# Placing a merge's output weights in a weight ring, splitting the first loads, and adding products of constants

## The chip, the cores and the metric

The kernel runs on one core of a Trainium2 chip. The metric is the device time of one execution in microseconds; before the change the median of three runs is 1440.2 us (1438.92 to 1441.64).

## The reference

One step of a decoder layer for 256 prompt tokens and 8 sample tokens (T = 264), width 1024, all in float32. What matters here are the end of the mixing part and the expert part:

```
h = rms_norm(x);  y_a = rwkv(h);  y_b = sparse_attention(h);  g_a, g_b = sigmoid gates of h
x = x + (g_a * (y_a @ w_br_a) + g_b * (y_b @ w_br_b)) @ w_out          # the merge
logits = rms_norm(x) @ w_router + b_router                             # 32 experts
top_val, top_e = top_k(logits, 4);  top_w = softmax(top_val)
for each expert e, over its tokens:
    u = h @ w_up[e] + b_up[e]                                          # 1024 x 2048
    y = clamped_swiglu(u) @ w_down[e] + b_down[e]                      # 1024 x 1024
    x += top_w * y
y = rms_norm(x)
```

The weights of an expert are 8 MiB (upper) and 4 MiB (lower); all 32 experts are always computed, on tiles of 64 token slots.

## The kernel before

The program is a row of blocks that end with a barrier of all engines: the input projection and the RWKV part, the attention (its setup, L928; the prompt, L1199; the samples, L1433), the merge (L1680) and the experts (L2099), with the routing at their head. Inside a block each engine has its own instruction stream, in program order, and waits on semaphores.

*The ring.* Expert weights go through eight buffers `pairs[0..7]` of 2 MiB (L175). Pairs 0 to 3 take the upper weights (two of the eight row tiles of 128 each), pairs 4 and 5 the lower weights of even experts, 6 and 7 those of odd experts. Pairs 4 to 7 lie in memory that is `sel` before: there the sample attention has its selected rows, and then the merge has the branch weights `w_br_a` and `w_br_b` in one half of the columns (0:128) and `w_out` in the other (128:256). All weight loads are issued by SP on one queue. `upper_weights(sp, 0)` (L183) issues the upper pairs of expert 0 in the merge; `down(0)` and `down(1)` (L1854) issue the lower pairs of experts 0 and 1 in the next block, behind the bias rows (L1858, L1859). From then on SP issues the upper pairs of expert e (L2110) as PE uses those of e-1, pair by pair (`up_used`, and `up_done` for the last), and the lower pairs (L2121) in the same way. The first issue of this kind, for expert 1, waits until PE has used pair 0 of expert 0.

*The merge.* SP issues eight loads of `w_out` (row c to `sel[:, c, ..., 128:256]`, in runs of 128 columns, 512 bytes), x again (L1702), seven constants (L1708) and the upper weights. POOL waits for all but the last of these and then issues the copy of the window cache, 4088 KB from HBM to HBM (L1718). PE computes the two branch products for eight column tiles (L1764, semaphore `ab`), then the output product (L1776, semaphore `od`) with x added through `twice` (L1778), then two sums for the router and the mean squares (L1784, L1789). DVE makes `mixed` (L1741 to L1743), the squares (L1749) and the last copy (L1751).

*The routing.* PE: two groups of products with `fold` (L2014), the transposes of all rows of x (L2022), the ranks (L2028, L2030), the first expert's rows picked by a product (L2036), the slot tables (L2043). DVE: logits, top 4, one-hot tables, `first_rows` (L1923), a wait for the bias rows and then the picked columns (L1931, L1932), and the gains of the first expert's rows (L1958). ACT writes the rows to a scratch tensor in HBM, 1.08 MB in all (L1879), from which POOL gathers each later expert's rows (L2161). Nothing of the first expert's upper product (L2417 bias, L2430 weights) waits for a gather.

*The experts.* PE does the upper product of e, the sums of e-1 or e-2 back onto the tokens (L2405), transposes of the next rows (L2387) and of h (L2393), the lower product (L2444 bias, L2451 weights). Up to expert 15 the lower product of e-1 stands behind the upper product of e, from 16 on that of e itself.

*Other places of the diff.* At the end of the RWKV part PE turns the last state (L896). In the attention's setup it transposes blocks of the cache (L1175), computes small setup products (L1146), the hidden layer of the compression (L1135), and after a wait for ACT's gelu the second layer (L1188, L1193). The attention of the prompt begins with 32 small products (L1347) and gate projections (L1356).

Of the kernel before, what the change touches and what calls it, by code (L numbers as in the profile page):

```python
# [29 lines left out]
P = 128  # L30
D = 1024
# [73 lines left out]
def build(nc, a, o, scratch):  # L105
    ctx = ExitStack()
    with ctx:
# [17 lines left out]
        def at(name, shape, place, dt=F32):  # L125
            return nc.alloc_sbuf_tensor_at(name, shape, dt, offset=place)
# [56 lines left out]
        def upper_weights(sp, e):  # L183
            for q in range(4):
                sp.dma_start(pairs[q][:], a["w_up"][0][e, 256 * q:256 * q + 256, :].rearrange("(p c) n -> p c n", c=2)).then_inc(ring_in[2 * q], 16)

# [31 lines left out]
        halves_of = (slice(0, HD), slice(HD, P))  # L218

# [403 lines left out]
        def rwkv_chunks(ar, q, bk, wc, av, br, vt, ktt, r, v):  # L623

            with nc.Block() as block, ExitStack() as st:
# [145 lines left out]
                def _(pe):  # L771
# [125 lines left out]
                    mm.then_inc(so, 1)  # L897

# [26 lines left out]
        def compress(sel, rows, qg, yb, B0, B1, gtok, bin_):  # L925

            with nc.Block() as block, ExitStack() as st:  # L928
# [196 lines left out]
                def _(pe):  # L1125
# [40 lines left out]
                    for b in range(NR // 2):  # L1166
                        if b % 2 == 0:
                            pe.wait_ge(C["raw_in"][b // 2], 32)
                        for r in (2 * b, 2 * b + 1):
                            if r >= 3:  # L1170
                                pe.wait_ge((fl_a, fl_d)[(r - 3) % 2], 2 * ((r - 3) // 2) + 1)
                            for kv in range(2):
                                for t in range(2):
                                    c0 = 256 * (r % 4) + P * kv
                                    mm = nc.tensor.transpose(banks[r % 3][:, TP * kv + P * t:TP * kv + P * t + P], raw[b // 2][:, t, c0:c0 + P], ident)  # L1175
                            mm.then_inc(turned, 1)
                        if 2 * b in at_half:
                            setup(at_half.index(2 * b))
                        if b:
                            layer1(2 * b - 2)  # L1180
                            layer1(2 * b - 1)
                        if 2 * b + 1 in at_half:
                            setup(at_half.index(2 * b + 1))
                    layer1(NR - 2)
                    layer1(NR - 1)
                    pe.wait_ge(gl_ok, 2)
# [7 lines left out]
                    mm.then_inc(vc, 1)  # L1194

# [482 lines left out]
        def merge(sel, br_in):  # L1678

            with nc.Block() as block, ExitStack() as st:  # L1680
# [11 lines left out]
                root_w = at("table_of_root", [P, 1], TEMPS)  # L1692
                wo_in, x_again = sem("mg_w_out_in"), sem("x_in_again")

                @block.sync
                def _(sp):
                    for c in range(KD):
                        sp.dma_start(sel[:, c, :, :, P:256], a["w_out"][0][P * c:P * c + P, :].rearrange("p (a b n) -> p a b n", a=2, b=4)).then_inc(wo_in, 16)
# [11 lines left out]
                    upper_weights(sp, 0)  # L1710
# [43 lines left out]
                def _(pe):  # L1754
# [15 lines left out]
                    for m in range(KD):  # L1770
                        if m >= 2:
                            pe.wait_ge(oe, m - 1)
                        for c in range(KD):
                            if m == 0 and c == KD - 1:
                                pe.wait_ge(mix_ok, KD)
                            mmul(banks[m % 2][:, 0:T], sel[:, c, m // 4, m % 4, P:256], mix[:, c, :], start=(c == 0), stop=False)  # L1776
# [13 lines left out]
                    mm.then_inc(partd, 1)  # L1790

# [24 lines left out]
        def route(st):  # L1816
# [33 lines left out]
            def sp_routes(sp):  # L1850
                def down(e):
                    for j in range(2):
                        slot = 8 + 4 * e + 2 * j
                        sp.dma_start(pairs[slot // 2][:], a["w_down"][0][e, 512 * j:512 * j + 512, :].rearrange("(p b c) n -> p b (c n)", b=2, c=2)).then_inc(ring_in[slot], 16)  # L1854

# [5 lines left out]
                down(0)  # L1861
                down(1)
# [147 lines left out]
            def pe_routes(pe):  # L2010
                mmul = nc.tensor.matmul
                for lo, signal in ((1, msd), (0, lgd)):
# [3 lines left out]
                    mm.then_inc(signal, 1)  # L2016
                for i in range(6):
# [13 lines left out]
                mm.then_inc(rkd, 1)  # L2031
                for t, (_, n) in enumerate(TILES):
# [543 lines left out]
```

## Time and profile before

| | |
|---|---|
| median of three runs | 1440.2 us |
| profiled execution, its own time | 1438.5 us |
| its span | 1436.6 us |
| PE busy | 1336.5 us, 93% of the span |
| DVE / ACT / POOL busy | 495.3 / 189.9 / 101.9 us |
| mean granted clock of TensorE | 0.974 |
| DMA | 479.94 MB, mean 334 GB/s |
| chain that ended last | DMA 33% (all of it upper weights of the ring), PE 32% |

The span reaches from the first to the last instruction; the execution's own time also holds what lies around it. The granted clock is a share of full speed: 1.00 is 2.4 GHz and 0.50 is 1.2 GHz. The chain is followed back from the last instruction, at each step to what released it. A busy share is a mean over stages with different limits, so the stages are read one by one. A matmul or a transpose of float32 operands takes several passes; the trace counts a product as two instructions and a transpose as one.

### The profile page before, as it was taken

Reading aid. Unit: us, or ns where it says so; the run is one execution under the profiler, and the core shown is the slowest. Engines: PE = TensorE matmul, PEld = TensorE weight load, DVE = VectorE, ACT = ScalarE, POOL = GpSimd, SP = SyncE. Lnnn points to the kernel's source line nnn. Section 1 sums busy time; section 2 is a strip of 40 time slices with the busy share of each in tenths; the row PEclk is TensorE's granted clock in tenths of the full one; section 3 lists DMA queues with packets and bytes.
Section 4 is the critical chain, followed back from the end, with each engine's and each line's share of the span. In section 5 each row is a group of like instructions: output and inputs, shape, how many; then the busy total and the mean of one; then the engine's idle time right before and its main releaser. Section 6 shows DMA issues by size and latency. Waiting matters only on the chain.

```text
span 1436.6 us, 20588 instructions
## 1 busy us (share of the span) xinstructions
PE 1336.5 (93%) x8365; PEld 663.5 (46%) x8366; DVE 495.3 (34%) x1055; ACT 189.9 (13%) x407; POOL 101.9 (7%) x150
## 2 busy tenths in 40 slices
PE   6998879899999989999999999999999999999995
PEld 6887867687778523332333233333333333233231
DVE  3455556424551413232323223224222322233224
ACT  3221113323410300000000000000000000000001
POOL 1002032330000000000000000000000000000000
PEclk9999989899999999999999999999999999999998
DMA  6333248184488899999999999999999999999993
GB/s 213 118 93 91 64 108 269 41 276 146 150 215 341 337 431 429 431 430 431 431 431 431 431 431 432 430 430 431 431 429 433 430 432 431 431 432 430 431 431 133
DMA packets 94195, 479.94 MB, mean 334 GB/s; under 512 B 12740, under 2 KB 61110, under 8 KB 69176
## 3 DMA queue, kind: packets, MB, share of 16 engines
q1 hardware_dynamic: 85832, 452.00, 77.7%
q0 software_dynamic: 7600, 25.45, 4.9%
q10 hardware_dynamic: 704, 1.63, 0.3%
q8 instruction: 46, 0.75, 0.2%
q14 instruction: 13, 0.11, 0.0%
HBM read 478.60 MB, written 8.56 MB: 339 GB/s over the span
## 4 chain that ended last, share of the span: by engine, by line
DMA 33%; PE 32%; DVE 1%; issue 1%; ACT 0%; SPq 0%; DVEq 0%; ACTq 0%
DMA ring<-in_w_up 33%; PE bank L2430 18%; PE bank L2451 7%; PE bank L2405 2%; PE bank L2444 1%; PE bank L2417 1%; DVE x L2268 1%; PE bank L2387 1%; PE bank L2036 0%; PE bank L2022 0%; PE bank L2393 0%; DVE ring L2356 0%; PE bank L2043 0%; DVE x L2365 0%; PE bank L2014 0%
## 5 line engine op out<-in xcount | busy, mean ns | idle before, releaser
L2430 PE MATMUL bank<-ring,ex_work 128*64 128x512 f32 x2048 | 464.9, 603 | 24.4 <-DMA ring<-in_w_up 24.4
L2430 PEld LDWEIGHTS bank<-ring,ex_work 128*64 128x64 f32 x2048 | 140.9, 138 | 333.9 <-issue 274.3
L2451 PE MATMUL bank<-ring,ex_work 128*64 128x512 f32 x1024 | 233.6, 610 | 0.0
L2279 DVE TENSOR_SCALAR ex_work<-bank 128x512 f32<-128x512 f32 x32 | 22.1, 691 | 401.6 <-PE bank L2430 401.6
L2268 DVE TENSOR_TENSOR x<-bank,x 128x512 f32<-128x512 f32 (+1 forms) x192 | 117.2, 670 | 101.5 <-PE bank L2405 101.5
L2451 PEld LDWEIGHTS bank<-ring,ex_work 128*64 128x64 f32 x1024 | 72.2, 140 | 159.1 <-issue 159.1
L2405 PE MATMUL bank<-ex_work,ex_back 64*128 64x512 f32 x384 | 91.1, 606 | 1.5 <-ACT ex_work L2199 1.5
L558 PE MATMUL bank<-hT,w_group 128*128 128x264 f32 (+1 forms) x400 | 90.1, 387 | 0.0
L558 PEld LDWEIGHTS bank<-hT,w_group 128*128 128x128 f32 (+1 forms) x400 | 74.3, 186 | 14.7 <-issue 0.7
L2161 POOL DMA_INDIRECT ex_work<-scratch_h,ex_si x31 | 31.7, 1022 | 603.1 <-PE bank L2387 602.3
L2193 ACT ACTIVATE ex_work<-ex_work 128x512 f32<-128x512 f32 x32 | 20.1, 629 | 382.0 <-DVE ex_work L2279 382.0
L1356 PE MATMUL bank<-hT,w_cmp 128*128 128x264 f32 x256 | 67.8, 410 | 0.0
L2275 DVE COPY ex_pick_down<-ex_pick 64x64 f32 (+1 forms) x31 | 5.8, 187 | 162.4 <-PE bank L2451 162.4
L2405 PEld LDWEIGHTS bank<-ex_work,ex_back 64*128 64x128 f32 x384 | 34.4, 186 | 57.8 <-issue 49.8
L2199 ACT ACTIVATE ex_work<-bank 128x512 f32<-128x512 f32 x32 | 19.1, 597 | 262.8 <-PE bank L2451 262.8
L1356 PEld LDWEIGHTS bank<-hT,w_cmp 128*128 128x128 f32 x256 | 48.8, 201 | 7.4
L2189 ACT ACTIVATE ex_work<-bank 128x512 f32<-128x512 f32 x32 | 19.1, 597 | 227.4 <-PE bank L2393 227.4
L2444 PE MATMUL bank<-ex_bias,ex_pick_down 32*64 32x512 f32 x128 | 34.4, 612 | 15.9 <-DVE x L2268 14.5
L2417 PE MATMUL bank<-ex_bias,ex_pick_up 32*64 32x512 f32 x256 | 34.8, 612 | 0.6 <-DVE ex_pick_up L2271 0.6
L1776 PE MATMUL bank<-mixed,sel_rows 128*128 128x264 f32 x128 | 30.4, 391 | 0.0
L2387 PEld LDWEIGHTS bank<-masks,ex_work 128*128 128x128 f32 x124 | 17.3, 208 | 26.3 <-issue 23.5
L1958 DVE TENSOR_TENSOR ex_work<-bank,gain_columns 128x256 f32<-128x256 f32 x64 | 23.9, 413 | 9.5 <-PE bank L2387 8.0
(485 smaller groups left out, 1180.8 us busy)
## 6 DMA issues: line engine op xcount, KB each, us to landing
ring<-in_w_up SPq DMA_DIRECT2D x128, 2048.0 KB, 24.1
ring<-in_w_down SPq DMA_DIRECT2D x64, 2048.0 KB, 26.8
w_group<-in_w_in SPq DMA_DIRECT2D x12, 1024.0 KB, 5.3
w_cmp<-in_w_in SPq DMA_DIRECT2D x8, 1024.0 KB, 8.7
sel_rows<-in_w_out SPq DMA_DIRECT2D x8, 512.0 KB, 7.3
out_win_s<-in_state_win_kv POOLq DMA_DIRECT2D x1, 4088.0 KB, 28.9
x<-in_x_prompt SPq DMA_DIRECT2D x4, 512.0 KB, 4.9
win_rows<-in_state_win_kv SPq DMA_DIRECT2D x4, 512.0 KB, 4.9
```

The lines of the kernel that those rows point to most:

```text
L558: mm = mmul(banks[2 + i % 4][0:n, 0:T], w[:, g % 3, kc, c:c + n], hT[:, kc, :], start=(kc == 0), stop=(kc == KD - 1))
L1356: mm = mmul(gate_bank(t)[:, 0:T], w[:, t // 2 % 2, kc, P * (t % 2):P * (t % 2) + P], C["hT"][:, kc, :], start=(kc == 0), stop=(kc == KD - 1))
L1776: mmul(banks[m % 2][:, 0:T], sel[:, c, m // 4, m % 4, P:256], mix[:, c, :], start=(c == 0), stop=False)
L1958: ins = nc.vector.tensor_tensor(B["xT"][:, :, gs], bank.rearrange("p (k s) -> p k s", k=4)[:, :, gs], R["gcol"][:, 2 * g:2 * g + 2].rearra ...
L2161: pool.indirect_dma_start(B["xg"][:], None, halves(scratch["h"]), bass.IndirectOffsetOnAxis(ap=B["si"][:, 0:1], axis=0), bounds_check=last ...
L2268: nc.vector.tensor_tensor(dst, banks[bank][0:n, :], dst, ALU.add).then_inc(S["added"], 1)
L2387: mm = nc.tensor.transpose(banks[6][:, P * k:P * k + P], B["xg"][:, 256 * (k // 2):256 * (k // 2) + 256].rearrange("s (p c) -> s c p", c=2 ...
L2405: mm = mmul(banks[bank], B["back"][hs, P * t:P * t + P], B["y"][hs, :], start=True, stop=True)
L2417: mmul(banks[n // 2][lo:lo + SLOTS, :], B["pick_up"][es, :], B["bias"][es, 512 * n:512 * n + 512], start=True, stop=False)
L2430: mm = mmul(banks[n // 2][lo:lo + SLOTS, :], B["xT"][:, k % 4, SLOTS * (k // 4):SLOTS * (k // 4) + SLOTS], slot_of(k)[:, 512 * n:512 * n + ...
L2444: mmul(banks[4][SLOTS * n:SLOTS * n + SLOTS, :], B["pick_down"][0:NEXP, :], B["bias"][0:NEXP, 2 * FF + 512 * n:2 * FF + 512 * n + 512], st ...
L2451: mm = mmul(banks[4][SLOTS * n:SLOTS * n + SLOTS, :], B["hT"][:, k % 4, SLOTS * (k // 4):SLOTS * (k // 4) + SLOTS], slot_of(8 + 4 * half + ...
```

## The change

`w_out` goes into pairs 2 and 3 of the ring, four row tiles each, one row of 1024 columns (4 KB) to a partition. With that `sel` holds only the branch weights, and SP issues, after the constants, the upper pairs 0 and 1 of expert 0, then, after a wait for the last branch product (`ab`), the lower pairs of experts 0 and 1, and after a wait for the last output product (`od`) the upper pairs 2 and 3. The two `down` calls of the next block are gone. Besides, `filled(bank, n)` issues on PE n products of the identity with 256 columns of constants into a bank that nobody reads then, at seven places.

```diff
-        def upper_weights(sp, e):
-            for q in range(4):
+        def upper_weights(sp, e, parts):
+            for q in parts:
                 sp.dma_start(pairs[q][:], ...).then_inc(ring_in[2 * q], 16)
+        def lower_weights(sp, e):
+            for j in range(2):
+                slot = 8 + 4 * e + 2 * j
+                sp.dma_start(pairs[slot // 2][:], a["w_down"][0][e, 512 * j:512 * j + 512, :].rearrange("(p b c) n -> p b (c n)", b=2, c=2)).then_inc(ring_in[slot], 16)
+        def filled(bank, n):
+            for _ in range(n):
+                nc.tensor.matmul(bank[:, 0:2 * P], ident, masks[:, 0:2 * P], start=True, stop=True)
...
@@ end of the RWKV part, behind L897 @@
+                    filled(banks[6], 4)
@@ attention's setup: behind the transposes of b == 1 (L1176); behind L1185; behind L1194 @@
+                        if b == 1:
+                            filled(banks[3], 2)
+                    filled(banks[2], 4)
+                    filled(banks[2], 2)
@@ merge @@
+                def wo(c):
+                    return pairs[2 + c // 4][:, c % 4 // 2, D * (c % 2):D * (c % 2) + D]
-                        sp.dma_start(sel[:, c, :, :, P:256], a["w_out"][0][P * c:P * c + P, :].rearrange("p (a b n) -> p a b n", a=2, b=4)).then_inc(wo_in, 16)
+                        sp.dma_start(wo(c), a["w_out"][0][P * c:P * c + P, :]).then_inc(wo_in, 16)
...
-                    upper_weights(sp, 0)
+                    upper_weights(sp, 0, (0, 1))
+                    sp.wait_ge(ab, KD)
+                    for e in range(2):
+                        lower_weights(sp, e)
+                    sp.wait_ge(od, KD)
+                    upper_weights(sp, 0, (2, 3))
...
-                            mmul(banks[m % 2][:, 0:T], sel[:, c, m // 4, m % 4, P:256], mix[:, c, :], start=(c == 0), stop=False)
+                            mmul(banks[m % 2][:, 0:T], wo(c)[:, P * m:P * m + P], mix[:, c, :], start=(c == 0), stop=False)
@@ merge, behind the last sum (L1790) @@
+                    filled(banks[7], 1)
@@ routing, SP @@
-                down(0)
-                down(1)
@@ routing, PE: ahead of the transposes (L2017); ahead of the wait for first_rows (behind L2031) @@
+                filled(banks[6], 2)
+                filled(banks[6], 2)
```

## Rows read from the trace of the kernel before

**Rows 1.** First line of the page.

```profile
span 1436.6 us, 20588 instructions
```

**Rows 2.** Windows by stage: busy us of each engine, granted clock, DMA share, GB/s.

```profile
416.00:430.00 14.00, 14.00 (x64) 11.85 (x63) 6.45 (x15) 0.00 (x0) 0.00 (x0) 1.00 1.15 296
440.00:456.00 16.00, 16.00 (x85) 14.05 (x85) 1.73 (x4) 1.56 (x4) 0.00 (x0) 1.00 1.05 449
456.00:474.00 18.00, 17.07 (x113) 14.51 (x111) 2.16 (x5) 1.96 (x5) 0.00 (x0) 1.00 0.49 210
477.00:496.30 19.30, 18.35 (x105) 10.72 (x105) 14.84 (x56) 9.28 (x17) 0.00 (x0) 0.83 1.02 372
525.80:1405.00 879.20, 840.68 (x3882) 278.75 (x3884) 235.69 (x481) 55.31 (x91) 34.68 (x57) 0.99 1.01 431
```

**Rows 3.** The chain in order of time: start us, us, what.

```profile
506.62 19.16 DMA ring<-in_w_up
...
649.06 3.68 PE bank L2430 x16
...
678.54 3.68 PE bank L2430 x16
...
983.77 13.88 PE bank L2430 x64
...
1011.66 13.88 PE bank L2430 x64
```

**Rows 4.** Timeline, issues of SP: start us, us of issuing, line, tile, count.

```profile
435.58 2.67 SPq L185 DMA_DIRECT2D ring<-in_w_up  x4
...
477.53 1.85 SPq L1854 DMA_DIRECT2D ring<-in_w_down  x4
...
496.32 33.67 SPq L2110 DMA_DIRECT2D ring<-in_w_up  x8
```

**Rows 5.** Timeline, PE and DVE from the merge's end to expert 1: start us, us.

```profile
473.11 0.43 DVE L1751 COPY logit_parts<-bank 128x264 f32<-128x264 f32 x1 [1.15 <-PE bank L1789]
...
476.30 4.51 PE L2022 MATMUL bank<-masks,x_T 128*128 128x128 f32 x24
...
480.67 1.22 PE L2028 MATMUL bank<-assigned,masks 128*128 128x32 f32 x12
...
483.73 4.53 PE L2036 MATMUL bank<-ex_work,first_rows 128*64 128x512 f32 x12 [0.95 <-DVE first_rows L1923]
...
487.02 0.18 DVE L1931 COPY ex_pick_up<-ex_pick 64x64 f32<-64x64 f32 x1
...
489.92 0.76 DVE L1958 TENSOR_TENSOR ex_work<-bank,gain_columns 128x256 f32<-128x256 f32 x2 [1.47 <-PE bank L2050]
...
509.75 1.09 PE L2417 MATMUL bank<-ex_bias,ex_pick_up 32*64 32x512 f32 x8 [0.56 <-DVE ex_pick_up L2271]
...
511.04 8.78 PE L2430 MATMUL bank<-ring,ex_work 128*64 128x512 f32 x32 [0.20 <-DMA ring<-in_w_up]
```

**Rows 6.** Landings of the weight pairs, 192 of them: least, median, most.

```profile
DMA to landing us min/median/max: 7.8/24.6/42.6
```

**Rows 7.** Timeline, PE ahead of the merge: start us, us, [idle before <-releaser].

```profile
200.38 3.53 PE L1175 MATMUL bank<-masks,x 128*128 128x128 f32 x16 [3.61 <-PEq L120]
...
210.53 1.97 PE L1175 MATMUL bank<-masks,gates_T 128*128 128x128 f32 x8 [2.69 <-DMA gates_T<-in_cache_cmp_kv,block_rows]
...
269.08 0.67 PE L1188 MATMUL bank<-sel_rows,w_cmp 128*64 128x264 f32 x4 [2.14 <-ACT sel_rows L1040]
...
273.76 3.59 PE L1347 MATMUL bank<-KcT,pT 64*128 64x8 f32 x32 [2.51 <-PEq L928]
...
306.26 1.95 PE L1356 MATMUL bank<-hT,w_cmp 128*128 128x264 f32 x8
```

**Rows 8.** Windows of two stretches at half clock.

```profile
210.50:217.30 6.80, 6.77 (x24) 4.12 (x26) 5.94 (x7) 0.71 (x2) 5.58 (x5) 0.50 1.05 330
272.00:282.10 10.10, 8.34 (x43) 7.31 (x44) 1.92 (x8) 0.00 (x0) 3.58 (x19) 0.50 0.02 3
```

More of the change, by code:

```diff
@@ L1850, in sp_routes @@
             def sp_routes(sp):
[L1851 to L1854, printed above, removed]
                 for i in range(2):
```

## The prediction

> **What bounds the kernel now.** I read the page's first line, the windows by stage, then the chain in order of time, then the timeline of the 40 us before the first expert. The profiled execution has a span of 1436.6 us [rows 1] and its own time is 1438.5 us, so 1.9 us lie around the span; the median of the runs is 1440.2 us, 1.7 us above it. From 525.8 to 1405 us the DMA engines are full at 431 GB/s, while PE is busy 840.7 of 879.2 us [rows 2]. Both look like the bound. The chain separates them: once PE's early lag is used up, it goes from weight landing to weight landing, 29.5 us from one expert to the next (649.06 to 678.54), whereas where PE runs alone an expert takes 27.9 us (983.77 to 1011.66) [rows 3]. So the weight stream is the slower of the two by 1.6 us an expert, and PE follows it. The stream has no gap from 477 us on; the end of the kernel moves with the time at which that stream reaches the upper weights of expert 1, and with nothing else behind it.
>
> Ahead of it the stream is not full: 296 GB/s in the branch products of the merge, and from 456 to 474 us 210 GB/s at a DMA share of 0.49 [rows 2]. There the window copy runs alone, because SP issued the four upper pairs at 435.58 us and can issue the lower ones only in the next block, at 477.53 us [rows 4]. The upper weights of expert 1 are issued at 496.32 us [rows 4], when PE has used the first pair of expert 0, and queue behind what is left of the lower weights.
>
> **The change, part by part.** *Stream.* Left in the queue at 496.3: from 474.84 us SP issued 0.79 MB of bias and 8.39 MB of lower weights, and ACT 1.08 MB of rows, 10.3 MB; from 477 to 496.3 the engines moved 372 GB/s x 19.3 us = 7.2 MB [rows 2], and about 0.5 MB before; 2.6 MB remain, 6.0 us at 431 GB/s. The landings say the same: the first pair of expert 1 lets PE start at 511.04 us and the last at 525.8 [rows 3, 5], three steps of 2.097 MB / 431 GB/s = 4.87 us later. After the change the lower weights are gone by then and the queue is empty when SP issues. A pair alone in the queue lands in 7.8 us, the shortest row there is [rows 6]: 496.3 + 7.8 = 504.1, and the last 504.1 + 3 x 4.87 = 518.7 us instead of 525.8. Estimate: -7.0 us. From this point on the queue never empties, as before, so the stream keeps it.
>
> Does PE keep it? Not at once. PE's second expert can't start its products before 510.8: ahead of the first stand the bias products, which wait for DVE's pick until 509.75 and take 1.09 us [rows 5]. From there the 64 instructions of an upper product take 13.9 us [rows 3] and the turn of h some 0.6, so it is done at 525.4; it was done 3.65 us after the last landing, at 529.4. PE gains 4.0 us here, and the other 3 us come back over two experts at 1.6 us each, as it catches the stream. There are 30 to do it in.
>
> *Bytes of the merge.* New order of SP: output weights (4.19 MB), x (1.08), constants (0.9), upper pairs 0 and 1 (4.19), then after the wait for the last branch product (about 437 us) 8.39 MB of lower weights, beside POOL's copy of 4.19: 22.9 MB from 416 on. At 431 GB/s that is 53 us, done at 469 us; PE's last output product, which the next wait is for, ends at 471.0, 2 us ahead of the block's last copy [rows 5]. Then upper pairs 2 and 3: 471.1 + 7.8 + 4.9 = 483.8 us, and expert 0 reads pair 2 only at 492.6 + 7.0 = 499.6. Covered by 16 us. Queued behind that wait on SP are the end of the block and the bias loads. SP's two issues cost 0.67 us each (2.67 for four [rows 4]), to 472.5; the block ends with DVE's copy at 473.5 anyway [rows 5]. The bias rows, at 474.8 in the queue behind the pairs, land with 0.79 + 1.05 MB more at about 486 to 488. DVE takes them at 487.02 and then has 1.47 us of idle time at 489.92 [rows 5], so up to 488.5 costs nothing. This is the tightest cover of the change; cost 0, bounds 0 and the slow rival below. That the output weights now lie in the ring changes no instruction of PE.
>
> The output weights were written in pieces of 512 bytes, and the windows show a DMA share of 1.15, full, at only 296 GB/s [rows 2]; the weights of the experts, whose rows are longer, move at 431 at the same share. I take 431 for the new rows of 4 KB. The Trainium skill ("DMA: Bandwidth & Descriptors", Specifications) holds that 512 bytes are enough for line rate; the trace disagrees. By the page the 296 would have another cause than the pieces, and the new rows would run into it too: 4.5 us more for these bytes, and the bias rows would land at 490 to 492, a cost of 2 to 4 us.
>
> *Fills before the merge.* A fill is a 128x128 product on 256 columns. Four of 264 columns are 8 instructions of 1.95 us together at full clock [rows 7], so a fill costs 0.47 us, and twice that at half clock. The four behind the state product stand in PE's wait for the block's end, 3.6 us before 200.38; the two in the second pair of blocks stand before the wait for rel_bias and then for the gathers, which leave PE idle 2.7 us before 210.53 [rows 7]: they cost 0, and what clock they save there goes into that wait, gain 0. The four before the hidden products (1.9 us in a wait of 2.14 before 269.08) and the two behind them stand ahead of a place that matters: the clock falls at about 272, after these waits, and is granted at 0.50 (1.2 GHz) to 282.1 us, with PE busy 8.3 us [rows 8]. The first 3.6 us of that are 32 small products [rows 7]; the rest, from 277.3 to 282.1, is dense work that would take 2.4 us less at 2.4 GHz. Bounds: 0, or +1.5 if the clock is already low when the fills run and they stick out of the wait, to 2.4 + 1.8 = 4.2 gained. A wait of 1.5 us and the small products stay, so I take half: -2.0 us.
>
> *Fills in merge and routing.* One at the merge's end, beside DVE's copy: 0. Two right ahead of the row transposes delay them by 0.95 us; the 24 transposes took 4.51 us [rows 5]; eight took 1.97 at half clock [rows 7, 8], so at full clock 24 take 3.0, and DVE's assignment, which PE needs next, comes 4.4 us after their start [rows 5]. At full clock the fills are covered, at half clock they cost up to 1.9. Two more stand in the 0.95 us before the first-row products at 483.73, which took 4.53 us and would take some 1.6 less had the clock not fallen [rows 5]. Bounds +1.9 and -1.9; I take +0.5: ahead of this stretch stands the block's end, 1.8 us of wait of which one fill covers only a quarter.
>
> Everything ahead of 492.6 counts fully, since the stream now waits for PE there. Sum: -7.0 - 2.0 + 0.5 = -8.5 us: 1430.0 for this execution, 1431.7 us for the median.
>
> **Rivals.** (a) *The fills buy no clock.* For it: the clock was at half from 210.5 on, after a wait of 2.7 us with dense products ahead of it [rows 7, 8], and waits remain beside each fill. Then -7.0 plus 0.5: 1433.7 us. (b) *The fills hold the clock everywhere*: -7.0 - 4.2 - 1.9 = -13.1, 1427.1 us. (c) *PE is the bound and never gets back the 3 us*: -4.0 - 1.5, 1434.7 us; against it stands the 1.6 us an expert. (d) *Slower: the merge's queue is too full.* If the 22.9 MB move at the 296 GB/s seen from 416 to 430, they take 77 us and end at 493; the upper pairs 2 and 3 and the bias rows stand behind them and the bias lands 22 us after its time, near 510 instead of 488. PE's first expert waits for it: +21.5 - 7.0 - 1.5 = +13, 1453 us. It decides from a bias landing past 488.5 + 8.5 = 497, that is a mean rate under about 355 GB/s. Against it: 449 GB/s from 440 to 456 [rows 2], with the copy in it. (e) In between, the same at 372 GB/s: bias at 495, which eats the gain: 1438 to 1441.
>
> **How the numbers follow.** A measurement of this kernel tells about 0.2%, 2.9 us, from no change. Forecast 0.54, (a) 0.18, (b) 0.11, (c) 0.08, (d) 0.04, (e) 0.05. Faster is all but (d) and (e): 0.91; same 0.05; slower 0.04. The range reaches from (b) with 1 us for the uncertain landing, 1426.5, past (c) with late bias rows, 1436.5.
>
> **What would show it.** Right: lower pairs issued near 437 us, DMA share near 1 from 440 to 470, a gap of the stream between 486 and 496 us, PE's expert 1 waiting less for weights and landing-bound again some 60 us later than 625; granted clock above 0.50 somewhere in 272 to 282. Wrong: DVE waiting for the bias rows after 488, PE waiting in expert 0, the stream's rate below 431, or a distance from expert 0's start to the end that shrinks by clearly less than 7 us.

## The result, and the profile after

The changed kernel takes 1443.98 us (median of 12 runs, 1439.67 to 1448.02), the kernel before on the same chip 1438.93 us (12 runs, 1435.47 to 1441.94): a ratio of 1.0039, 95% interval 1.0026 to 1.0052. It is slower by 5 us, where 8.5 us less were forecast: outside the range, and the other way. The profiled execution has 1444.07 us, almost the median, so its trace can stand for the kernel. Most of the forecast's single steps can be found in it, and one new wait that is larger than all of them together.

First the page's first line, and the windows of the stages (us, busy us of PE, PEld, DVE, ACT, POOL with instructions, granted clock, DMA share, GB/s), to be laid beside [rows 1, 2, 8]:

```profile
span 1442.2 us, 20656 instructions
```

```profile
414.00:426.00 12.00, 12.00 (x56) 10.13 (x55) 5.97 (x15) 0.00 (x0) 0.00 (x0) 1.00 1.02 412
430.00:440.00 10.00, 10.00 (x50) 8.64 (x49) 3.17 (x8) 0.39 (x1) 0.68 (x1) 1.00 1.03 427
440.00:456.00 16.00, 16.00 (x84) 14.02 (x83) 1.57 (x4) 1.17 (x3) 0.00 (x0) 1.00 0.99 427
456.00:474.00 18.00, 16.68 (x114) 13.99 (x112) 2.69 (x10) 1.96 (x5) 0.00 (x0) 1.00 0.69 280
477.00:496.30 19.30, 11.96 (x80) 8.77 (x78) 7.22 (x19) 8.19 (x15) 0.00 (x0) 0.85 0.81 265
492.30:506.00 13.70, 5.95 (x18) 1.53 (x20) 5.53 (x25) 0.00 (x0) 1.82 (x3) 0.50 0.21 77
272.00:282.10 10.10, 8.37 (x68) 6.55 (x67) 4.71 (x14) 1.20 (x4) 6.32 (x22) 1.00 0.01 2
525.80:1405.00 879.20, 842.87 (x3894) 279.92 (x3893) 235.69 (x481) 55.90 (x92) 34.96 (x58) 0.99 1.01 431
```

Three forecasts hold here: the output weights move at 412 GB/s instead of 296 (431 was put), the stretch from 272 us is granted 1.00 instead of 0.50, and the experts' stream still runs at 431. But from 456 to 474 us, where the queue was to be full until 469, the share is 0.69, and between 477 and 496.3 PE is busy for only 11.96 us instead of 18.35. What it waits for stands in the timelines: SP's issues, then DVE, then PE.

```profile
428.11 1.18 SPq L185 DMA_DIRECT2D ring<-in_w_up  x2
435.28 1.84 SPq L190 DMA_DIRECT2D ring<-in_w_down  x4
469.01 0.80 SPq L185 DMA_DIRECT2D ring<-in_w_up  x2
...
475.15 0.47 SPq L1878 DMA_DIRECT2D ex_pick<-in_c_pick  x1
507.64 0.35 SPq L2128 DMA_DIRECT2D ring<-in_w_up  x1
```

```profile
499.75 0.19 DVE L1947 COPY ex_pick_up<-ex_pick 64x64 f32<-64x64 f32 x1 [13.82 <-DMA ex_pick<-in_c_pick]
```

```profile
482.61 2.94 PE L2054 MATMUL bank<-ex_work,first_rows 128*64 128x512 f32 x12
...
486.93 2.03 PE L2061 MATMUL bank<-cells,x_T 128*128 128x64 f32 x16
500.00 1.98 PE L2435 MATMUL bank<-ex_bias,ex_pick_up 32*64 32x512 f32 x8 [11.03 <-DVE ex_pick_up L1947]
502.04 2.83 PE L2448 MATMUL bank<-ring,ex_work 128*64 128x512 f32 x6
```

Up to the routing SP issues its weights within 2 us of the times that were forecast (lower pairs at 435.28 for 437, upper pairs 2 and 3 at 469.01 for 471). The pick matrix, last of the bias rows, is issued at 475.15 and DVE copies it only at 499.75, after a wait of 13.82 us; in the kernel before it did so at 487.02 without one [rows 5]. PE is through with the slot products at 488.96, stands for 11.03 us, and does the first bias products at half clock: 1.98 us instead of 1.09. From 492.3 to 506 us, 13.7 us, the granted clock is 0.50. The chain says the same (start us, us, what):

```profile
475.15 24.58 DMA ex_pick<-in_c_pick
501.23 0.77 DVE ex_work L1974 x2
502.04 15.89 PE bank L2448 x64
...
685.07 3.61 PE bank L2448 x16
688.83 25.21 DMA ring<-in_w_up
```

The first landing of weights on it after the bias is at 688.83 + 25.21 = 714, where before PE followed the stream from 625 us on (DMA from 625.03 to 649.01 on its chain).

**Four marks.** The end can be followed through four marks of any of these kernels: the first weight product; SP's issue of the first upper pair of expert 1 (L2110 before, L2128 after); the landing of the last of expert 1's four upper pairs; and the end of the span. The landings here and below are the semaphore increments that the trace records.

```
                    before    after
first product        492.6    502.0    +9.4
issue                496.3    507.6    +1.9 more
last pair landed     525.8    531.5    -5.6 (29.5 us after issue, then 23.9)
end                 1436.6   1442.2     0   (910.8 and 910.7 us after the landing)
```

+9.4 + 1.9 - 5.6 = +5.7 us, the difference of the spans (5.6). The moved loads did take 5.6 us out of the stream. The late bias rows put 11.3 us in front of it.

### The profile page after: what moved, and what is told of

It reads as the page before. It is cut to its first block, busy times and chain, and to the rows that moved or that the text cites. A ratio compares the mean times of both kernels' runs of the same rounds, so it can differ in the third digit from the quotient of the medians.

```text
span 1442.2 us, 20656 instructions
## 1 busy us (share of the span) xinstructions
PE 1340.8 (93%) x8399; PEld 665.3 (46%) x8400; DVE 494.7 (34%) x1055; ACT 189.6 (13%) x407; POOL 101.7 (7%) x150
## 4 chain that ended last, share of the span: by engine, by line
PE 35%; DMA 30%; DVE 2%; issue 1%; SPq 0%; ACT 0%; DVEq 0%; ACTq 0%
DMA ring<-in_w_up 28%; PE bank L2448 20%; PE bank L2469 8%; PE bank L2423 3%; DMA ex_pick<-in_c_pick 2%; PE bank L2462 1%; PE bank L2435 1%; PE bank L2405 1%; DVE x L2286 1%; PE bank L2411 0%; DVE ring L2374 0%; DVE x L2383 0%; DVE ex_work L1974 0%; DVE ex_work L2301 0%; DVE ex_work L2304 0%
## 5 line engine op out<-in xcount | busy, mean ns | idle before, releaser
L2435 PE MATMUL bank<-ex_bias,ex_pick_up 32*64 32x512 f32 x256 | 35.7, 627 | 13.5 <-DVE ex_pick_up L1947 11.0
L1798 PE MATMUL bank<-mixed,ring 128*128 128x264 f32 x128 | 30.4, 391 | 0.0
L1974 DVE TENSOR_TENSOR ex_work<-bank,gain_columns 128x256 f32<-128x256 f32 x64 | 23.9, 413 | 8.1 <-PE bank L2405 8.1
```

The costliest lines, as they stand in the source:

```text
L1798: mmul(banks[m % 2][:, 0:T], wo(c)[:, P * m:P * m + P], mix[:, c, :], start=(c == 0), stop=False)
L1974: ins = nc.vector.tensor_tensor(B["xT"][:, :, gs], bank.rearrange("p (k s) -> p k s", k=4)[:, :, gs], R["gcol"][:, 2 * g:2 * g + 2].rearra ...
L2435: mmul(banks[n // 2][lo:lo + SLOTS, :], B["pick_up"][es, :], B["bias"][es, 512 * n:512 * n + 512], start=True, stop=False)
```

## Why the rows are late: landings by engine

The trace has sixteen increments of its semaphore for each load, as many as the core has DMA engines; they are read here as one for each engine. The increments of the trace of before and after, in groups (us):

```
                 before                          after
window copy      8 at 447.9-448.4, 8 at 467.1-468.1    8 at 440.5-440.8, 8 at 459.4-460.6
upper pair 0    16 at 442.6-443.4                     16 at 435.1-439.5
upper pair 1     8 at 447.6-448.3, 8 at 464.4-467.9    8 at 440.1-440.5, 8 at 456.9-461.1
upper pair 2     8 at 452.4-453.1, 8 at 471.7-472.8    8 at 476.6-476.9, 8 at 487.5-490.3
upper pair 3     8 at 457.3-457.9, 8 at 476.8-480.4    8 at 482.1-484.8, 8 at 494.2-496.4
lower pair 4    16 at 486.6-489.4                      8 at 444.9-445.3, 8 at 464.2-466.0
lower pair 7    16, the last at 506.0                  8 at 459.5-461.1, 8 at 479.0-480.8
bias and pick   96 at 478.1-483.9                     48 at 483.8-490.5, 48 at 495.4-499.7
```

From the window copy on, every load comes in two halves of eight engines some 19 us apart. The copy's tensors have eight batches as their slowest dimension, and eight engines carry it: 4.19 MB / 8 = 0.52 MB each, at 431 / 16 = 26.9 GB/s for an engine 19.4 us. Before the change, the eight without a share of it raise its semaphore at 447.9 to 448.4, together with that of upper pair 1, and go straight on with the weights. A load has landed when its last engine has, so from there on one half of the engines is 19 us behind, and the other runs ahead and is idle once its share is done. Upper pair 1 shows that it is not only loads behind the copy that wait: after the change SP issues it at 428.58, 3 us ahead of the copy (POOL, 431.70), and its second half lands at 456.9 to 461.1, beside the copy's. The Trainium skill ("DMA: Bandwidth & Descriptors", Why a DMA increments its semaphore by 16 and not by 1) says that the number of engines is the largest number up to 16 that divides the slowest dimension of both sides; the trace agrees for a slowest dimension of 8, by the two groups of eight.

That was to be seen before the change. The DMA view of the kernel before, 456 to 474 us, gives by queue: packets, MB, share of the 16 engines.

```profile
DMA packets 188, 3.78 MB, mean 210 GB/s; under 512 B 32, under 2 KB 32, under 8 KB 32
...
q1 hardware_dynamic: 154, 2.13, 27.7%
q0 software_dynamic: 33, 1.64, 21.0%
```

Together that is 48.7% of sixteen engines, 7.8 of them. The share of 0.49 that the prediction read as "the window copy runs alone" is in the main eight full engines (from 458 to 474 us the rate is 216 GB/s, half of 431), with more of the weights' bytes (2.13 MB, q1) than of the copy's (1.64 MB, q0). The other eight had nothing left after 457.9 us.

With that the merge after the change can be worked out. The slower half has half of the 18.7 MB of queued loads and the whole copy: 9.35 + 4.19 = 13.54 MB at 215 GB/s = 63 us, from 414 us, where the output weights begin to move, to 477; lower pair 7 is there at 479.0 to 480.8. The upper pairs 2 and 3, issued at 469.01, start on that half only then, 9.7 us for their half of the 4.19 MB; the bias rows, with the rows of h that ACT stores meanwhile, 1.9 MB more, 4.3 us: 494. The last one came at 499.7; the 5 us between are not accounted for.

## The experiments

Two causes are mixed here: eight of the engines are late, and the two upper pairs stand ahead of the bias rows in SP's queue. The rival is that neither matters and the loss comes from PE: fills in the way, or a lower clock. Each experiment was timed beside the kernel before, which had medians of 1438.93 (beside the changed kernel), 1439.94, 1439.95 and 1440.36 us in the four sets. A difference of medians across sets, such as 1443.98 - 1437.87 below, is therefore uncertain by more than 1 us, and the ratios and the traces are the better witnesses.

**No fills.** In the changed kernel:

```diff
-            for _ in range(n):
+            for _ in range(0):
                 nc.tensor.matmul(bank[:, 0:2 * P], ident, masks[:, 0:2 * P], start=True, stop=True)
```

> The changed kernel without any of its products of constants. Theory Q (queue): the changed kernel is late because the bias rows of the experts stand on SP's queue behind 12.6 MB of weights, and eight of the sixteen DMA engines reach them only near 499 us since they also carry the window copy; the fills have nothing to do with it. Then the first expert's weight products start at about 502 to 504 us again and the time is that of the changed kernel or 1 to 3 us more (1444 to 1447 us), as the fills gave about 2 us ahead of the merge. Rival F (fills): the fills stand in the way of the transposes and of the first rows and cost more than they give; then the time falls to 1438 us or less.

Measured: 1447.83 us (before 1439.94, ratio 1.0043, 1.0028 to 1.0059). The first product is at 505.5 us, the last pair lands at 535.3. Without its fills the kernel is no faster, so they don't cause the loss. Nor does a lower clock: from 477 to 496.3 us it is granted at 0.85 in the changed kernel and at 0.83 before. Whether they take something off it the times don't show: the medians are 3.9 us apart, but the ratios, 1.0043 and 1.0039 (1.0026 to 1.0052), overlap almost wholly. In the traces the difference lies ahead of the merge, which begins at 415.90 us here (SP's first issue of the output weights) and at 411.81 in the changed kernel; from there to the end it is 1030.0 and 1030.4 us.

**Bias rows in another queue.** POOL, which has nothing to do here, issues them at the start of its part of the block:

```diff
             def sp_routes(sp):
-                for i in range(2):
-                    es = slice(NEXP * i, NEXP * i + NEXP)
-                    sp.dma_start(B["bias"][es, 0:2 * FF], a["b_up"][0]).then_inc(S["bias_in"], 16)
...
             def pool_routes(pool):
+                for i in range(2):
+                    es = slice(NEXP * i, NEXP * i + NEXP)
+                    pool.dma_start(B["bias"][es, 0:2 * FF], a["b_up"][0]).then_inc(S["bias_in"], 16)
...
```

> The changed kernel with the six loads of bias rows and pick table issued by POOL on its own queue instead of by SP. Theory Q: they no longer stand behind the weights, land by about 484 us, DVE's wait of 13.8 us and PE's of 11.0 us are gone and the first expert's weight products start at 490 to 492 us instead of 502.0; the time is 9 to 12 us under the changed kernel, 1432 to 1435 us. Rival P (pairs): pairs 2 and 3 themselves, issued only at 469 us, come too late (they landed at 490 and 496), so PE waits for them inside expert 0 and only 4 to 6 us are won, 1438 to 1440 us.

Measured: 1437.87 us (before 1439.94, ratio 0.9985, 0.9971 to 0.9999). That is the time of the rival P, but not by its reason: the 64 instructions of expert 0's upper product run from 495.04 to 510.58 with no wait for a pair. The timeline of DVE:

```profile
492.75 0.19 DVE L1943 COPY ex_pick_up<-ex_pick 64x64 f32<-64x64 f32 x1 [7.69 <-DMA ex_pick<-in_c_pick]
```

The place in the queue alone, with the same bytes and the same engines, takes 6.1 us off by the medians (1443.98 - 1437.87), and the ratio goes from 1.0039 to 0.9985. The rows now overtake upper pair 3, whose last increment is at 498.6. The Trainium skill ("DMA: Bandwidth & Descriptors", Queues, rings and completion order) has each engine take turns between its queues packet by packet; the trace agrees, rows issued 4 to 7 us after the pair (468.5; 472.58 to 475.06) land 6 us ahead of it. A wait of 7.69 us stays; the likely reason is that the rows still share eight late engines (the second half of lower pair 7 lands at 481.1 to 484.0), but this queue was not run with a spread copy.

**The copy in sixteen pieces.** The same bytes, cut so that the slowest dimension is 16:

```diff
-                    pool.dma_start(o["win_s"][0, :, 0:511].rearrange("b t a g d -> b (t a g d)"),
-                                   a["state_win_kv"][0, :, 1:512].rearrange("b t a g d -> b (t a g d)")).then_inc(win_copied, 16)
+                    pool.dma_start(o["win_s"][0, :, 0:511].rearrange("b t a g d -> b (t a g d)").rearrange("b (s x) -> s b x", s=16),
+                                   a["state_win_kv"][0, :, 1:512].rearrange("b t a g d -> b (t a g d)").rearrange("b (s x) -> s b x", s=16)).then_inc(win_copied, 16)
```

> The changed kernel with the window copy cut into 16 pieces of the slowest dimension instead of 8. Theory C (copy on half the engines): the copy ran on eight engines and cost each of them 4.19 MB / 8 at 27 GB/s, 19.4 us; on sixteen it costs each 9.7 us. Then all sixteen increments of a weight pair come within 1 us of each other, the bias rows land about 9 to 10 us sooner, at 490 us, the first expert's products start at 492 to 493, and the time is 7 to 10 us under the changed kernel, 1434 to 1437 us. If the landings stay split in two groups 19 us apart, the copy is not their cause and the time stays at 1444.

Measured: 1434.77 us (before 1439.94, ratio 0.9971, 0.9953 to 0.9988), 9.2 us below the changed kernel, and below the kernel before too. The two groups are gone: lower pair 4 has sixteen increments from 455.2 to 457.7, lower pair 7 from 469.8 to 472.7. The windows, and the copy of the pick:

```profile
440.00:456.00 16.00, 16.00 (x85) 14.07 (x84) 1.40 (x4) 1.56 (x4) 0.00 (x0) 1.00 0.99 382
456.00:474.00 18.00, 16.68 (x112) 13.91 (x112) 3.07 (x13) 2.34 (x6) 0.00 (x0) 1.00 0.99 404
```

```profile
489.79 0.26 DVE L1947 COPY ex_pick_up<-ex_pick 64x64 f32<-64x64 f32 x1 [4.70 <-DMA ex_pick<-in_c_pick]
490.10 1.09 PE L2435 MATMUL bank<-ex_bias,ex_pick_up 32*64 32x512 f32 x8 [1.98 <-DVE ex_pick_up L1947]
```

From 456 to 474 us the share is 0.99 instead of 0.69. The wait of 13.82 us is 4.70 us, and the lower pairs are done at 472.7, the 469 of the prediction give or take 4. This is the step that was missing in it.

**Bias rows ahead of the upper pairs.** The changed kernel, with pairs 2 and 3 issued behind the bias rows, without the wait for the last output product:

```diff
-                    sp.wait_ge(od, KD)
-                    upper_weights(sp, 0, (2, 3))
...
                     sp.dma_start(B["pick"][es, :], a["c_pick"]).then_inc(S["bias_in"], 16)
+                upper_weights(sp, 0, (2, 3))
```

> The changed kernel with the upper pairs 2 and 3 of expert 0 issued behind the bias rows, in the experts' block (some 7 us later), and with no wait for the output products. Theory Q: the bias rows then stand behind the lower weights alone, land by about 484 to 486 us, and DVE's 13.8 us wait is gone; pairs 2 and 3 land on the engines of the copy at about 496 us, just when expert 0 comes to them. First weight product at 490 to 492 us, time 1432 to 1436 us. Rival P: pairs 2 and 3 are late for expert 0, PE waits inside it and the time is 1438 us or more.

Measured: 1435.51 us (before 1439.95, ratio 0.9973, 0.9958 to 0.9987). Each of the two edits alone brings about the same time (0.9973 and 0.9971), but this one does not do away with DVE's wait:

```profile
492.31 0.19 DVE L1946 COPY ex_pick_up<-ex_pick 64x64 f32<-64x64 f32 x1 [4.46 <-DMA ex_pick<-in_c_pick]
```

The rows' increments run from 478.9 to 492.3, beside lower pair 7, whose second half lands at 485.6 to 487.5 on the late engines. The expectation of 484 to 486 for the rows was wrong here.

**Both edits.**

> The changed kernel with the window copy in sixteen pieces and upper pairs 2 and 3 of expert 0 issued behind the bias rows. Theory (the loss of the change is the late bias rows, by the copy's eight slow engines and by the two pairs ahead of the rows): DVE takes its first bias row without a wait for DMA, the first weight product stands at 490 to 491 us of the span, 938.8 us lie from there to the end as in the two kernels that have one of the edits, span about 1429.5, median 1431 to 1433, ratio 0.9945 to 0.9960, below both kernels that have one edit. Rival (the two edits cure the same us): no better than either alone, median 1434.5 to 1436.

Measured: 1430.43 us (7 runs, 1427.22 to 1432.93; before 1440.36; ratio 0.9930, 0.9904 to 0.9955). Its median is below both single edits (the intervals of the ratios just touch for the sixteen pieces, 0.9953 to 0.9988), and DVE has no wait for a DMA any more. SP and PE:

```profile
477.83 0.42 SPq L1876 DMA_DIRECT2D ex_pick<-in_c_pick  x1
478.29 1.95 SPq L185 DMA_DIRECT2D ring<-in_w_up  x2
496.47 10.63 SPq L2127 DMA_DIRECT2D ring<-in_w_up  x4
```

```profile
488.34 1.10 PE L2060 MATMUL bank<-cells,x_T 128*128 128x64 f32 x8
489.80 2.03 PE L2060 MATMUL bank<-cells,x_T 128*128 128x64 f32 x16
491.76 1.09 PE L2434 MATMUL bank<-ex_bias,ex_pick_up 32*64 32x512 f32 x8
492.78 13.95 PE L2447 MATMUL bank<-ring,ex_work 128*64 128x512 f32 x64
```

The bias products follow the slot products at once, at full clock (1.09 us), and the rows are complete at 483.0. This kernel has the lowest median of all here, 10 us below the one before: the change as it was meant.

**The changed kernel without the copy.** One row of the window is still copied, so the rest of that output is left out and 4.2 MB are not moved.

```diff
-                    pool.dma_start(o["win_s"][0, :, 0:511].rearrange("b t a g d -> b (t a g d)"),
-                                   a["state_win_kv"][0, :, 1:512].rearrange("b t a g d -> b (t a g d)")).then_inc(win_copied, 16)
+                    pool.dma_start(o["win_s"][0, 0:1, 0:1].rearrange("b t a g d -> b (t a g d)"),
+                                   a["state_win_kv"][0, 0:1, 1:2].rearrange("b t a g d -> b (t a g d)")).then_inc(win_copied, 16)
```

> The changed kernel without the window copy (one row of it is left), so 4.2 MB less to move, and the window output is left out. Theory (the eight engines that carry the copy hold up every weight pair behind it): lower pairs land in sixteen increments close together, bias rows land by 485, no wait of DVE for them, first weight product at 490 to 491, distance to the end 938.8 as with the sixteen-piece copy, median 1431 to 1433. Rival (the bytes, not their spread, made the rows late): then this kernel is clearly below the one with both edits, by some us.

Measured: 1433.47 us (before 1440.36, ratio 0.9960, 0.9941 to 0.9978). Against the copy in sixteen pieces (0.9971, 0.9953 to 0.9988) that is no clear difference: once the copy is spread, its 4.2 MB cost next to nothing here. What was expected wrongly was that the rows would be there by 485 without a wait: their last increment is at 491.3, and DVE waits 3.33 us:

```profile
456.00:474.00 18.00, 17.63 (x114) 14.76 (x112) 2.17 (x5) 1.95 (x5) 0.00 (x0) 1.00 0.46 174
```

```profile
491.29 0.42 DVE L1947 COPY ex_pick_up<-ex_pick 64x64 f32<-64x64 f32 x1 [3.33 <-DMA ex_pick<-in_c_pick]
```

The queue ran dry ahead of 474 (share 0.46), the lower pairs were all there at 464.0, and still the rows are late. What is left is the two upper pairs ahead of them, issued just before, 4.19 MB or 9.7 us. So the queue place has a price of its own, even without the copy.

**Controls on the kernel before.** The fills alone (the same seven places), the sixteen pieces alone, and both:

> The kernel before with the products of constants alone, at the same seven places. Theory: they lift the clock ahead of the merge and in the first-row products and give 1 to 3 us, 1436 to 1438 us, since the start of the weight stream moves with PE only in part (the lower weights are issued when the merge ends, so the whole stream moves with it). Rival F: they cost, 1439 to 1441 us.

> The kernel before with the window copy in 16 pieces. Theory C: in the kernel before, the eight engines of the copy end with the upper pairs at 476.8 us, just when the lower weights are issued, so nothing waits for them; spreading the copy moves landings of pairs that nobody waits for: same time as the kernel before within 2 us. If it gives 5 us or more, the copy already cost the kernel before something that I haven't seen.

> The kernel before with the fills and the copy in sixteen pieces, weights as before: the control of the run above. Theory: the copy's engines matter there only by the half-used stretch ahead of the routing; first weight product at 490, 941.4 us to the end as in the kernel before with the sixteen-piece copy, median about 1434.5. The moved loads are then worth 2.6 us by the distance to the end. Rival (sixteen pieces are worth nothing without the moved loads): median 1436 as with the fills alone, distance 944.

Measured: fills 1436.18 us (ratio 0.9980, 0.9966 to 0.9995); sixteen pieces 1439.51 (0.9993, 0.9980 to 1.0005); both 1437.45 (0.9984, 0.9965 to 1.0002). In the old order the spread of the copy matters to nothing that can be measured, where the late half was done with the upper pairs at 480.4, 7 us before DVE took up the bias rows; and beside the fills it adds nothing. The value of 941.4 us from the first product to the end, seen with sixteen pieces alone and expected again with both, did not come back (944.0). The moved loads themselves are the step from this last control to both edits: 0.9984 to 0.9930, intervals that don't overlap, 7.0 us by the medians. By the two traces it is only 1.7 us (spans 1432.5 and 1430.8); but the control's profiled execution, 1434.46 us, was 3.0 below its median and that of the other, 1432.73, 2.3 above, which is the other 5.3. The merge also begins at different times in the two traces, 411.13 and 414.51 us, behind the same code; from there to the end it is 1021.3 and 1016.3 us, 5.0 apart. So the moved loads gave 5 to 7 us, and a plain difference of two spans can be off by more than 3.

**The copy early.** If the copy is in the way in the merge, it can go where the DMA engines are idle: POOL issues it (in sixteen pieces) near 172 us, in the RWKV part.

```diff
+                    pool.wait_ge(C["w_in"], 96)
+                    pool.dma_start(o["win_s"][0, :, 0:511].rearrange("b t a g d -> b (t a g d)").rearrange("b (s x) -> s b x", s=16),
+                                   a["state_win_kv"][0, :, 1:512].rearrange("b t a g d -> b (t a g d)").rearrange("b (s x) -> s b x", s=16)).then_inc(win_copied, 16)
...
-                    pool.dma_start(o["win_s"][0, :, 0:511].rearrange("b t a g d -> b (t a g d)"),
-                                   a["state_win_kv"][0, :, 1:512].rearrange("b t a g d -> b (t a g d)")).then_inc(win_copied, 16)
```

> The changed kernel with the window copy issued by POOL at the end of the RWKV part, where the DMA engines are nearly idle, in 16 pieces. Theory C: the merge's queue then holds only the weights; lower weights land by 462 us, pairs 2 and 3 by 480, the bias rows by 485, in one group of engines. No wait for the bias rows; first weight product at 490 us; time 1431 to 1434 us, at or under the kernel with the copy in 16 pieces (1434.8). If the stream's gain is real, the distance from the first weight product to the end is 937 to 940 us, against 943.9 in the kernel before.

> The kernel before with the products of constants and with the copy issued at the end of the RWKV part, but with the weights issued as before (lower weights behind the merge). It tells what the moved loads alone are worth once the copy is out of the way. Theory: the same first weight product (490 us) as with the moved loads, but the upper weights of expert 1 stand behind 2 to 3 MB of lower weights and land 4 to 7 us later against it: 4 to 6 us above the changed kernel with the early copy, 1436 to 1438 us, no different from the fills alone (1436.2). Rival: the moved loads are worth nothing and both kernels take the same time.

Both expectations were wrong. On the changed kernel 1440.13 us (before 1439.95, ratio 0.9997, 0.9979 to 1.0015); on the kernel before with the fills 1444.28 (1.0036, 1.0020 to 1.0052), 8 us above the fills alone. The routing is shorter for it in the first one, 18.4 us from the routing's first product to the first weight product instead of 29.1, but the routing starts 10 us later, at 482.9 instead of 472.9. The loss stands right behind the copy's issue. PE, in the first of the two:

```profile
177.48 1.15 PE L809 MATMUL bank<-m_Y,m_level_wu 64*64 64x64 f32 x32 [1.35 <-issue]
...
185.56 0.80 PE L862 MATMUL bank<-v_tok,kt_tok 64*64 64x64 f32 x10 [3.53 <-issue]
...
186.26 6.15 PE L872 MATMUL bank<-at_tok_av,m_Y 64*64 64x128 f32 x63
```

```profile
186.00:192.50 6.50, 6.50 (x84) 6.50 (x82) 0.05 (x1) 1.02 (x1) 0.00 (x0) 0.59 0.01 3
```

In the changed kernel it is granted at 1.00 there. The second kernel has the same hole at the same products (4.35 us, ahead of 184.17). From 171 to 196 us PE is busy 20.13 us; in the changed kernel, with no copy there, 23.44 us. From the first product of `v_tok` and `kt_tok` (180.2 us here) to the last of the products that turn the state it takes 24.6 and 24.0 us in these two kernels, and 18.1 us in all eleven others: 6.5 and 5.9 us of loss in this stretch alone. The rest of the 10 us is within what the start of the merge varies by otherwise. That the copy holds up PE's own instruction fetch is the nearest reading, as it comes twice with the copy and never without; it was not tested by itself.

## Why the prediction was wrong

- **"22.9 MB ... At 431 GB/s that is 53 us, done at 469 us", cost 0.** This step failed, the rate and with it the overlap of the copy that was put at no cost. It spread the copy over sixteen engines. Eight of them had 13.5 MB to carry at 215 GB/s, until 479.0 to 480.8; the mean over all bytes, from 414 to 480.8 us, is 22.9 MB / 66.8 us = 343 GB/s. Spreading the copy brings the lower pairs to 472.7 and takes 9.2 us off. The row against it lay in [rows 2], the share of 0.49, and was read as one transfer alone, not by queues and by the number of engines.
- **"the bias rows ... land ... at about 486 to 488"**, "the tightest cover of the change". They landed at 499.7. The sum had put 4.19 MB of upper weights ahead of them with no slack for a late queue. From SP's first issue of a bias row to the last landing the forecast had 13 us at most (474.8 to 488); without the copy it is 16.4 (474.90 to 491.3), with it 26.8 (472.89 to 499.7). So this step was off by 3 us by itself, and by 10 us more through the engines. The price of the wait was right: every us past 488.5 costs one, 499.7 - 488.5 = 11.2, and PE waited 11.03.
- **Rivals.** What happened is (d) and (e) in mechanism. (d) named the point, a mean rate under 355 GB/s or a landing past 497: 343 and 499.7 came out. It took the low rate from the stretch of the output weights, which was the wrong reason, and its evidence against, 449 GB/s from 440 to 456 us, is a rate of all engines before half of them ran out. Together they had 0.09. The times that went with them, 1453 and 1438 to 1441 us, were not met: (e) had the rows at 495 and a gain that is just used up.
- **A term that no case had.** The long wait leaves PE at half clock: granted 0.50 from 492.3 to 506, and SP issues the next pair 5.6 us after the first product instead of 3.7, as PE uses up the first pair slower. With both edits it is 3.7 again. That cost is 1.9 us, on top of the wait. It hardly depends on the length of the wait: with 1.98 us of PE's idle time (sixteen pieces) the issue still comes 5.1 us after the first product, with 6.41 us (no fills) 6.0.
- **Stream -7.0.** Right in kind, a bit too large. Issue to last landing is 23.9 us, forecast 22.4 (504.1 + 14.6 - 496.3): -5.6. The part that failed is the landing of a pair alone, put at the least of 192, 7.8 us [rows 6]; expert 1's first pair took 9.0 us (507.64 to 516.6), and 8.6 and 9.3 with sixteen pieces and with both edits. That it comes to PE over several experts is right: PE follows the stream again only from 714 us. And the end follows that last landing by 909.1 to 911.2 us in the traces of all thirteen kernels: the step "the stream keeps it" holds.
- **Output weights at 431 instead of 296 GB/s.** 412 at a share of 1.02, nearly so. By the rule of the Trainium skill that the prediction names ("DMA: Bandwidth & Descriptors", Specifications) the rate would not have changed with the pieces; it did.
- **Fills -1.5 together.** The sign is right where it can be seen: on the kernel before the ratio is 0.9980 (0.9966 to 0.9995), 0.7 to 4.9 us, which leaves the forecast possible; on the changed kernel the times don't tell. The traces give the parts. *Ahead of the merge* the clock is 1.00 from 272 to 282 as hoped; the merge begins at 411.81 us instead of 413.89, the forecast 2 us, but that is luck for a single pair: it begins at 413.7 to 415.9 in the three kernels without fills and at 410.9 to 414.5 in the eight with them (the early copy left aside), 2.1 us apart in the mean, with a spread that is larger. *In the routing* +0.5 was the wrong sign: from its first product to the end of the slot tables it is 16.8 us in the kernel before, 15.3 in the three kernels with fills and the old order, and 16.0 in the changed kernel. That is -1.5 and -0.8. The first-row products took 2.94 us instead of 4.53 [rows 5]; the row transposes, with two fills ahead of them, stayed slow in the changed kernel:

```profile
475.42 4.35 PE L2039 MATMUL bank<-masks,x_T 128*128 128x128 f32 x24
```

## What to carry over

Ask of every DMA how many engines carry it, and of every window with half a DMA share which queues and how many engines make it up; half a share can mean that half of the engines have no room at all, and each load that has a share on those waits for them. Where a queue is filled further ahead, sum the bytes by engine, and put the small loads that somebody needs next ahead of the large ones that nobody needs yet. In a kernel that ends in a full stream, follow one mark, the landing at which the stream takes over, and not only the time of one execution: here the end lay 910 us behind it, in every version.

## What had not been expected of the hardware

- A copy on eight of sixteen engines, issued on a queue of its own beside one in full flow, delays the loads beside and behind it by its whole length on those engines: two groups of eight increments 19 us apart over five loads, and 9 to 11 us apart at the upper pairs 2 and 3.
- Rows of 4 KB to a partition moved at 412 GB/s where pieces of 512 bytes moved at 296, with the DMA share at 1.0 or above in both [rows 2].
- A 4.19 MB copy beside small 64x64 products went with 3.3 us less busy time of PE in 25 us: holes of 3.53 and 4.35 us that nothing in the profile explains, and products that took longer behind them at a granted clock of 0.59. The stretch was 6 us longer in both kernels that had the copy there.
